# Retention: gate blocks projected before value rows, head normalisation moved into the first attention rounds

## What is computed

```python
q = rotary(q, pos, d, RET_ROT_BASE)
k = rotary(k, pos, d, RET_ROT_BASE) * (d ** -0.5)
inner = einsum(einsum(q, k) * dmat, v)            # dmat: causal decay, one table per head
o = inner + cross                                 # all 512 positions
ret = o * lax.rsqrt(mean(o * o, axis=-1, keepdims=True) + NORM_EPS)
ret_out = silu(rg) * ret.reshape(B, S, RET_W)
mix = sigmoid(gate_a) * (nsa_out @ w_proj_a) + sigmoid(gate_b) * (ret_out @ w_proj_b)
```

## Time and profile before

| what | value |
|---|---|
| median of 3 runs | 2154.61 us (2153.83 to 2157.46) |
| the profiled execution's own time | 2156.66 us |
| its span in the profile | 2154.6 us |
| PE busy | 2039.9 us (95%) |
| DVE, ACT, POOL busy | 921.2, 729.6, 798.3 us |
| mean granted clock of PE | 0.968 |
| chain that ended last | PE 66%, issue 17%, DVE 8%, POOL 5%, ACT 2% |

### The profile page before, as it was taken

One profiled execution on the slowest core, in us unless ns is written; L12 is line 12 of the kernel. 1 busy time (PEld: TensorE's weight loads), 2 busy tenths in 40 slices (PEclk: granted clock), 3 DMA queues, 4 the chain that ended last, 5 costly groups with the idle time before them and its releaser, 6 DMA issues.

```text
span 2154.6 us, 26069 instructions
## 1 busy us (share of the span) xinstructions
PE 2039.9 (95%) x9608; PEld 1606.4 (75%) x9608; DVE 921.2 (43%) x1351; ACT 729.6 (34%) x1210; POOL 798.3 (37%) x333
## 2 busy tenths in 40 slices
PE   7998799999899999979999998998899999999999
PEld 5777466588778888868878887775666877888887
DVE  5761455421763245265561113667872323111111
ACT  5232355532432133142213224445434333221221
POOL 3363321134255445414443442331022442444442
PEclk8999899999899999979999999999899998999999
DMA  5354111124367646624733332321022332343332
GB/s 160 88 128 106 32 44 36 40 72 119 104 189 188 173 130 184 194 59 124 191 101 94 100 99 59 78 69 40 11 50 59 88 98 68 97 100 96 96 91 67
DMA packets 156613, 211.16 MB, mean 98 GB/s; under 512 B 15432, under 2 KB 133736, under 8 KB 156392
## 3 DMA queue, kind: packets, MB, share of 16 engines
q1 hardware_dynamic: 140672, 166.37, 30.9%
q10 hardware_dynamic: 15848, 43.51, 6.8%
HBM read 206.69 MB, written 2.10 MB: 97 GB/s over the span
## 4 chain that ended last, share of the span: by engine, by line
PE 66%; issue 17%; DVE 8%; POOL 5%; ACT 2%; DMA 1%; ACTq 1%; POOLq 0%; DVEq 0%
PE ps L570 20%; PE ps L572 20%; PE ps L571 20%; POOL wlo L534 4%; DVE xT L2064 1%; DVE PT L2079 1%; PE ps L950 1%; DVE nmax L1947 1%; PE ps L994 1%; DMA trig<-in_ada_w 1%; DVE tmp L1811 1%; PE ps L603 0%; DVE Pb L2079 0%; PE ps L791 0%; PE ps L974 0%
## 5 line engine op out<-in xcount | busy, mean ns | idle before, releaser
L534 POOL TENSOR_TENSOR wlo<-raw,whi 128x1024 fp32r<-128x1024 f32 (+1 forms) x317 | 782.9, 2484 | 1310.4 <-ACT whi L1223 1281.8
L570 PE MATMUL ps<-hhi,whi 128*128 128x512 f32 x1488 | 598.7, 402 | 14.8 <-DVE hlo L1736 7.4
L571 PE MATMUL ps<-hlo,whi 128*128 128x512 f32 x1488 | 585.1, 393 | 0.0
L572 PE MATMUL ps<-hhi,wlo 128*128 128x512 f32 x1488 | 585.1, 393 | 0.0
L1223 ACT ACTIVATE whi<-raw 128x1024 fp32r<-128x1024 f32 x309 | 316.4, 1054 | 408.2 <-PE ps L572 393.2
L570 PEld LDWEIGHTS ps<-hhi,whi 128*128 128x128 f32 x1488 | 283.1, 190 | 89.0 <-issue 23.6
L572 PEld LDWEIGHTS ps<-hhi,wlo 128*128 128x128 f32 x1488 | 282.7, 190 | 60.6
L571 PEld LDWEIGHTS ps<-hlo,whi 128*128 128x128 f32 x1488 | 283.6, 191 | 55.9 <-issue 1.4
L570 PE MATMUL ps<-hidhi,whi 128*128 (+1 forms) x608 | 236.9, 390 | 3.0 <-DVE mod L2085 3.0
L571 PE MATMUL ps<-hidlo,whi 128*128 (+1 forms) x608 | 236.6, 389 | 0.0
L572 PE MATMUL ps<-hidhi,wlo 128*128 (+1 forms) x608 | 236.5, 389 | 0.0
(11 more groups left out here) (345 smaller groups left out, 2476.8 us busy)
## 6 DMA issues: line engine op xcount, KB each, us to landing
raw<-in_ffn_w SPq DMA_DIRECT2D x264, 256.0 KB, 3.8
raw<-in_w_in SPq DMA_DIRECT2D x154, 256.0 KB, 3.9
trig<-in_ada_w ACTq DMA_DIRECT2D x72, 512.0 KB, 4.6
raw<-in_w_up SPq DMA_DIRECT2D x64, 256.0 KB, 3.9
raw<-in_w_down SPq DMA_DIRECT2D x64, 256.0 KB, 3.9
raw<-in_w_out SPq DMA_DIRECT2D x32, 256.0 KB, 3.8
xrow<-in_x ACTq DMA_DIRECT2D x4, 512.0 KB, 6.6
raw<-in_cmp_k_w SPq DMA_DIRECT2D x8, 256.0 KB, 3.7
```

Of the source, the lines that this page charges most:

```text
L534: last = pool.tensor_tensor(lo, src, hi.bitcast(F32), ALU.subtract)
L570: pe.matmul(out_, lhi, rhi, start=first, stop=False)
L571: pe.matmul(out_, lhi, rlo, start=False, stop=False)
L572: return pe.matmul(out_, llo, rhi, start=False, stop=last)
```

## The change

- In the list of blocks the two gate blocks come before the two value blocks (the weights are loaded in that order too).
- The heads no longer share `st` and `PT`: head h is copied in place of its keys, `rkT[h]`, and its squares, root and reciprocal are in `SQ[h]`. The sum of squares goes into the head's own PSUM bank, 3 + h % 2, so the first product of heads 2 and 3 waits for the root of the head two before.
- The sum of head 3 is issued between the two score pairs of round 0.
- DVE takes only the reciprocal of head 0 in the retention, those of heads 1, 2 and 3 at the end of rounds 0, 1 and 2. ACT's `retention_high` comes in round 1 (head 0), round 2 (head 1) and round 3 (heads 2 and 3). The waits for `rt_done` ahead of the attention are gone; the one of `branch_b` in round 4 stays.
- The first four copies into `SQ` wait for POOL's multiplication with the reciprocal (`rt_m`), the first transpose for the fourth root.

The diff, without lines that only follow from these:

```diff
-    rvg = [("A", W1["rv"] + 256 * b, 128, ("rv", 256 * b)) for b in range(2)]
-    rvg += [("B", W1["rg"] + 256 * b, 128, False, [("silu", "srg", 2 * b + c) for c in range(2)]) for b in range(2)]
+    rvg = [("B", W1["rg"] + 256 * b, 128, False, [("silu", "srg", 2 * b + c) for c in range(2)]) for b in range(2)]
+    rvg += [("A", W1["rv"] + 256 * b, 128, ("rv", 256 * b)) for b in range(2)]
...
@@ POOL, retention @@
-                    r, o = PT[:, h % 2, :], st[:, h % 2, :]
+                    r, o = SQ[h], rkT[:, h, :]
...
@@ PE, retention @@
+            def head_sum(h):
+                pe.wait_ge(rt_ev, h + 1)
+                pe.matmul(ps[:, 3 + h % 2, :], cst[:, C_HD128:C_HD128 + P], SQ[h], start=True, stop=True).then_inc(rt_sum, 1)
...
                     if j == 0 and h >= 2:
-                        pe.wait_ge(rt_ev, h - 1)
+                        pe.wait_ge(rt_root, h - 1)
...
-                for x in range(16 + 3):
+                for x in range(16 + 2):
@@ PE, turn, and the middle of a round @@
+                        if u == 0:
+                            pe.wait_ge(rt_root, 4)
...
+                            if r == 0:
+                                head_sum(3)
                             score_pair(r, 1)
@@ PE, ahead of the attention @@
-            pe.wait_ge(rt_root, 4)
             nsa_attention()
@@ ACT, retention @@
                 for h in range(4):
                     sc.wait_ge(rt_pv, 4 * h + 4)
-                    if h >= 2:
-                        sc.wait_ge(rt_done, h - 1)
-                    sc.activation(st[:, h % 2, :], ps[:, 3 + h % 2, :], ACT.Copy)
-                    sc.activation(PT[:, h % 2, :], ps[:, 3 + h % 2, :], ACT.Square).then_inc(rt_ev, 1)
+                    sc.activation(rkT[:, h, :], ps[:, 3 + h % 2, :], ACT.Copy)
+                    sc.activation(SQ[h], ps[:, 3 + h % 2, :], ACT.Square).then_inc(rt_ev, 1)
                     sc.wait_ge(rt_sum, h + 1)
-                    sc.activation(PT[:, h % 2, :], ps[:, 5 + h % 2, :], ACT.Sqrt, bias=col(C_EPS)).then_inc(rt_root, 1)
-                    if h >= 1:
-                        retention_high(h - 1)
+                    sc.activation(SQ[h], ps[:, 3 + h % 2, :], ACT.Sqrt, bias=col(C_EPS)).then_inc(rt_root, 1)
@@ ACT, copy_turned, a round, and ahead of the attention @@
+                    else:
+                        sc.wait_ge(rt_m, t + 1)
...
+                    for h in {1: (0,), 2: (1,), 3: (2, 3)}.get(r, ()):
+                        retention_high(h)
...
             retention()
-            retention_high(3)
-            sc.wait_ge(rt_done, 4)
             nsa_attention()
@@ DVE, retention, and a round @@
-                        if j == 3 and h >= 1:
-                            finish(h - 1)
                         x += 1
-                finish(3)
+                retention_root(0)
+
+            def retention_root(h):
+                ve.wait_ge(rt_root, h + 1)
+                ve.reciprocal(SQ[h], SQ[h]).then_inc(rt_rcp, 1)
...
-                ve.wait_ge(rt_done, 4)
                 n = len(UNITS1)
...
                         maxima(r, 1)
+                        if r < 3:
+                            retention_root(r + 1)
```

More of the change, by code:

```diff
@@ L740, in retention @@
                                   start=True, stop=True).then_inc(rt_qk, 1)
-                    if 2 <= x < 18:
+                    if 2 <= x:
                         pv(x - 2)
-                    if x % NT == 2 and x >= 6:
+                    if x % NT == 2 and 6 <= x:
                         head_sum(x // NT - 1)
@@ L1354, in retention_high @@
                 sc.wait_ge(rt_o, h + 1)
-                sc.activation(O1["b"][0][:, h, :], st[:, h % 2, :], ACT.Copy).then_inc(rt_hi, 1)
+                sc.activation(O1["b"][0][:, h, :], rkT[:, h, :], ACT.Copy).then_inc(rt_hi, 1)
             def retention():
@@ L1817, in retention @@
             def retention():
-                def finish(h):
-                    ve.wait_ge(rt_root, h + 1)
-                    ve.reciprocal(PT[:, h % 2, :], PT[:, h % 2, :]).then_inc(rt_rcp, 1)
                 ve.wait_ge(pj_silu, 4)
```

## The result

The changed kernel took 2142.57 us in the median of five executions, the kernel before, run beside it, 2157.46 us (2153.83 to 2162.81). One of the five, of 7055 us, was disturbed; the other four took 2137.26 to 2146.18 us (2140.51 in the median), and the ratio uses these four. It is 0.9925, 95% interval 0.9907 to 0.9943: faster by 0.75%, about 16 us. I had forecast 4.2 us and a range that began at 2146.2, so the kernel came out faster than the whole range.

A forecast was written before the change was run, and what follows sets the result against it. PE, busy 95%, was taken as the bound. Terms +0.1, -1.8, -2.8 and the rounds brought round 4 6.15 us earlier; less 2.0 for clock, the gain was 4.2: 2154.61 to 2150.4 us, range 2146.2 to 2154.0.

The forecast's parts named there:

- Gate blocks first: Ahead of the retention: PE waits 1.4 us for the last gate, 1.35 less around `hidc`; clock holds, gaining 1.8.
- Sum +0.1: Net cost of the new block order ahead of the retention, before any clock effect: 0.1 us.
- The clock at the retention's start: Score products and first `pv` run at full clock, as the low stretch ahead shrinks from 3.2 to 1.8 us: gain 1.8.
- The two waits of 1.35 and 1.25: In the retention, PE's waits for decay products behind DVE reciprocals go: 2.8 us with refill, nothing following them.
- Round 0: Second score pair starts 5.5 us after the last `pv`; PE idles 2.5 us and the clock falls.
- Rival 3: Round 0's table load for Exp makes ACT stand about 1.4 us more: gain 2.8, about 2151.8 us, chance 0.04.
- Rounds 1 to 3, and what is late next: From round 0's second pair to the next ones 6.8, 5.45, 6.6 us, then 9.85 to `rt_done`, POOL and ACT in series.
- The stall of round 4: Ahead of round 4's branch b, PE waits 5.8 us for the last head's POOL and ACT chain.
- this clock term: Behind the new idle ahead of round 4's branch b, half of 4 us is lost to low clock: 2.0 us.
- rival 1: Better, about 2147.8 us: DVE not held by POOL, or clock not falling in round 0 or round 4's stall; chance 0.27.
- rival 2: Gain nearly eaten, about 2152.6 us: retention starts at half clock, or round 3's chain is 2 us longer; chance 0.16.
- rival 4: Slower, about 2157.5 us: clock stays at half until round 3's second pair, 7.1 us lost; chance 0.08.

The follow-up runs named there:

- experiment 3: Changed kernel, gate blocks first, with the second compression product and its guard moved from PSUM bank 0 to bank 2: 2151.36 us, ratio 0.9968 to the kernel before.
- experiment 2: Changed kernel with value blocks first again, so only the heads' part of the change: 2150.76 us, ratio 0.9975 to the kernel before.
- experiment 1: Kernel before with only the order edited, gate blocks ahead of value blocks, heads as before: 2145.61 us, ratio 0.9939.
- experiment 4: Changed kernel run once more without edits, on the chip of the first three follow-ups: 2141.46 us, ratio 0.9925 to the kernel before.
- experiment 5: Changed kernel with blocks of four banks waiting for each bank just ahead of its first matmul, in every projection: 2134.45 us, ratio 0.9892 to the kernel before.
- experiment 6: Changed kernel with POOL doing a head's two products before the previous head's subtraction, ACT's rounding moved to match: 2134.44 us, ratio 0.9913 to the kernel before.
- experiment 7: Changed kernel with both the bank-by-bank waits and the new POOL order: 2129.84 us, ratio 0.9873 to the kernel before.
- experiment 8: Kernel before, value blocks first, with only the bank-by-bank waits added: 2148.08 us, ratio 0.9956.
- lazy banks: Edit making four-bank blocks wait bank by bank: 2134.45 us on the changed kernel, 2129.84 with POOL's new order too, 2148.08 on the kernel before.

## Why the prediction was wrong

**The step that failed is "Gate blocks first", with its "Sum +0.1".** I had worked out its end: the stall behind the last gate (1.4 forecast, 1.38 measured), and what is left of the stretch ahead of the compression's small matmuls (0.95 forecast, 0.97 measured, from 207.47 to 208.44). Its beginning I had put at nothing without looking. I read PE's timeline from the end of the last projection on, and the claim that "12 to 15 us of idle or slow time can be had at most" counted only from there. The wait of 11.46 us was in the trace before, 50 us ahead, at the first instruction of the list that the diff reorders. I even had it in hand: the prediction prices half clock by the stretch "after 11 us idle" at 171 to 175, and never asks what that idle waits for or what the new order makes of it. In its place the runs showed:

- 10.69 us less idle (11.46 less the 0.77 for the slab that it had covered), by the bank: experiment 3 brings it back with gates first, experiment 2 with values first, and the kernels with gates first and the product in bank 0 (the changed one, experiments 1 and 4 to 7) are free of it.
- about 1.8 us for the half clock behind it (19 matmuls in 171 to 175, their starts 0.21 us apart, 0.12 at full clock).
- less 1.38 for the gate stall, and 1.33 back at `hidc` (1.84 to 0.51). 10.69 + 1.8 - 1.38 + 1.33 = 12.4, measured 12.48.

No rival had this either: the range reached only to errors of the terms I had.

**The clock at the retention's start.** I let it hold because the stretch ahead shrank. It held, and the retention took 20.63 us (20.4 forecast). The reason is not shown: experiments 2 and 8 hold it as well with the old 1.84 us idle, while the execution before dropped to 0.58. So my reason isn't borne out, and that the term came out is luck as far as the runs show. The 1.8 us are real in the two profiles compared; how much of them belongs to the change is open.

**The two waits of 1.35 and 1.25** for decay products went, as forecast, and nothing took their place, as forecast.

**Round 0.** The second pair came 5.48 us behind the last `pv` (5.5 forecast), its wait is 2.47 (2.5 forecast). ACT after the change:

```profile
233.04 0.69 ACT L1365 ACTIVATE PT<-ps,cst 128x512 f32<-128x512 f32 x1 [1.92 <-PE ps L720]
233.74 1.28 ACT L1383 ACT_TABLE_LOAD   x1
235.04 0.29 ACT L1383 ACTIVATE st<-ps,nmax 128x31 f32<-128x31 f32 x1
```

The load begins when the root ends and costs 1.28; the exponential follows at once. Rival 3, a drain of its own at this switch, is refuted here. The Trainium skill (ScalarE: Activation LUTs, "What ACT_TABLE_LOAD costs") adds a drain of about 1.38 us to every switch to another set of functions. This trace shows none; with it PE's wait, by estimate, would have been 3.9.

**Rounds 1 to 3, and what is late next.** 5.88 against 6.8 forecast, 5.22 against 5.45, 6.02 against 6.6, 9.36 against 9.85: the order and the releasers were right, the sum 2.24 too long. 0.9 of it is round 0 to 1, where I had taken the half clock for as long as it lasted before; it ended about 3 us after the fall. In experiment 2 it didn't fall, and that stretch from the last `pv` to round 4 is 31.0 instead of 31.96. DVE was held up beside POOL, as forecast; DVE's products of `normalise`, four at a time, after the change (128 x 128 twice, then 128 x 31):

```profile
246.54 1.88 DVE L1885 TENSOR_SCALAR tmp<-tmp,rcpg 128x128 f32<-128x128 f32 x4
...
252.63 1.97 DVE L1885 TENSOR_SCALAR trig<-trig,rcpg 128x128 f32<-128x128 f32 x4
...
257.30 2.69 DVE L1885 TENSOR_SCALAR st<-st,rcpg 128x31 f32<-128x31 f32 x4
```

With POOL idle, before the change, the first takes 0.87 and the last 0.68. So they are held by 1.0, 1.1 and 2.0; I had counted 1.1 twice, and the third doesn't lie on the chain that PE waits for. The Trainium skill (SBUF — State Buffer, "SBUF: two separate sides") calls the pair of ports that DVE and POOL share an exclusive lock that is held for a whole instruction. Holds of just under one POOL operation of 1.26, and of under two in the third row, agree with it; that the ports are the cause is not shown here.

The stall of round 4 was 5.12 (5.8 forecast). Its label names ACT's `gsig`, but the one that PE asks for here had been done at 250.5; who is late is seen on POOL, after the change:

```profile
255.98 1.27 POOL L554 TENSOR_TENSOR retlo<-rkT,rethi 128x512 fp32r<-128x512 f32 x1 [2.04 <-ACT rethi L1357]
257.20 1.26 POOL L549 TENSOR_TENSOR rkT<-rkT,PT 128x512 f32<-128x512 f32 x1
258.54 1.26 POOL L552 TENSOR_TENSOR rkT<-rkT,srg 128x512 f32<-128x512 f32 x1
260.54 1.26 POOL L554 TENSOR_TENSOR retlo<-rkT,rethi 128x512 fp32r<-128x512 f32 x1 [0.74 <-ACT rethi L1357]
```

Subtract, multiply, multiply, ACT's rounding, subtract, ending at 261.80, 0.15 ahead of PE: the chain as written down. Experiment 6 changes only its order and takes 4.2 of the 5.12. Behind the stall the clock cost 1.27 (2.0 forecast). Together the rounds and this clock term came out 3.0 better than forecast, about as much as one doubt of rival 1 gives, but its events didn't come: DVE was held up and the clock fell both times. Rivals 2 and 4 didn't come either.

Put together: by the ratios the heads gave 5.4 us where my terms for them make 2.45, and the order 13.2 where my terms for it make 1.7 (1.8 for the clock less 0.1).

## What to carry to other kernels

Where a diff reorders a list, read the trace at the first instruction of that list and at the last, and at every place where the list asks for a buffer: number the outputs of the old and of the new order and write the bank beside each. A wait often belongs to the number at which an item stands, not to what the item is, and a guard that asks for all buffers ahead of a block makes the block as late as the slowest of them. And list all waits over 1 us on the bounding engine in the whole stage before costing any edit: one such view would have shown the 11.5 at its top. Where an idle stretch serves as the price of something else, ask what it waits for. Where an edit stands in a shared helper, look up every place that calls it: the lazy banks gained at least as much outside the stage as inside it. And note how much a fix has to spare: this one has 0.5 us.

## What the hardware showed that I had not expected

- The granted clock isn't a function of one idle time. After 1.84 us idle at the same place it was 0.58 in the execution before and 1.00 in experiments 2 and 8; after 2.47 us idle in round 0 it fell in the changed kernel (0.66 over 236 to 241) and not in experiment 2 (1.00 over 250 to 256). Behind the 5.1, 7.6 and 11.5 us idle shown above it was at half each time, behind the 0.91 of experiment 6 it wasn't.
- Behind the first use of `rethi` the three kernels with lazy banks have the same work, and it took 1871.2 us in one execution and 1880.7 in another. Part of it was the granted clock of 260 to 385: 1.00 in the execution of experiment 8, 0.95 in that of experiment 5, by estimate (0.05 of 125 us) 6 of the 9.5 us.
- Long reciprocals on DVE took 3.34 us beside POOL operations as without them, while short products next to them were held by 1 to 2 us.
